# Reordering the last two expert pairs of a one-core diffusion trunk step: one residual on GpSimd, early return tiles, a split output tile

## The chip, the cores and the metric

The kernel runs on one core of a Trainium2 chip. A core has TensorE (matrix products into the eight banks of PSUM), VectorE, ScalarE, GpSimd and SyncE, each with its own queue of instructions, and 16 DMA engines that move data between the chip's memory and SBUF. The engines meet only at semaphores: an instruction raises one when it is done, and a wait in another queue holds that queue, and everything behind it, until the count is reached. The metric is the device time of one execution in microseconds, as the median of several runs; a profile is one execution more.

## The reference

One layer of a trunk over 384 tokens of width 1024: 128 context tokens and 256 latent tokens, each with its own condition. A mixer block (Fourier branch and retention branch) comes first, then the mixture of experts with which the changed code has to do, then a last norm:

```
x = x + g1 * mix
h = rmsnorm(x, norm2_g) * (1 + sc2) + sh2
x = x + g2 * moe(h)          # 64 experts of width 256, 8 chosen per token, and a shared one
y = rmsnorm(x, final_norm_g)
```

Here `g2` is a row of 1024 gates, one row for the context tokens and one for the latent tokens. An expert computes `(silu(t @ we_g) * (t @ we_u)) @ we_d` for the tokens that chose it, times their routing weight. All 64 experts are computed, and their weights (3 MB each) are read once. The outputs are `y` for both sets of tokens and the two retention states of the context.

## The kernel before

The tokens are three tiles of 128 rows (`TT = 3`): tile 0 is the context, tiles 1 and 2 are the latent tokens. `x` holds them in SBUF, 128 x 3 x 1024. The mixer and the routing take the first 370 us or so. Then the 64 experts go by in 32 pairs (`PAIRS = LAST = 32`, so the last two are pairs 30 and 31). The order of every engine's queue is written out by hand.

For a pair `p`, GpSimd gathers the tokens' rows from memory, TensorE turns them, and `gate_up(p)` multiplies them with the gate and up weights into bank 0. ScalarE takes the silu, VectorE multiplies it with the up half and the routing weight (`hidden`, `hid_ready`), TensorE turns the hidden rows into bank 1 (`hidden_T`), ScalarE copies them to SBUF (`hidT_ready`), and `down(p)` makes two halves of 512 columns in banks 2 and 3. The rows then go back to their tokens by products with a one-hot matrix `slotT`. So that this is exact enough, a row is split into a rounded high part `y_hi` (ScalarE, `hi_ready`) and a remainder `y_lo` (VectorE, `lo_ready`), and each of six return tiles (three token tiles, two column halves) is the sum of two matmuls, one for each part. For pairs 0 to 29 VectorE adds the six return tiles to `y_sum`, a buffer in `hTf` (`sums`, `summed`).

The last two pairs go another way. GpSimd gathers each slot's gate row (`gather_gates`), VectorE multiplies the down product with it (`remainder_gated`, which also forms the remainders), and the return tiles of both pairs accumulate in six banks (`LAST_BANKS = (4, 5, 6, 7, 0, 1)`, in the order of `LAST_TILES`: the three tiles' low halves, then their high halves). The last adds then go straight to `x` (`last_sums`). What pairs 0 to 29 left in `y_sum` is multiplied by the gate rows and added to `x` by `residual(t)`, two VectorE operations of 128x1024 for each token tile. The gate rows come by a DMA of SyncE's queue (`g2_rows_in`) behind the last weights.

The order on TensorE at the end is `gate_up(31)`, `hidden_T(31)`, the return of pair 30 (`scatter_two(30)`), `down(31)`, the return of pair 31 (`scatter_two(31)`). On VectorE it is `residual(0)`, the pair's weights, `hidden(31)`, `residual(1)`, `residual(2)`, `remainder_gated(31)`, then a load of the number of further rounds from SBUF with a branch on it (there are none for these inputs, so the `Else` side runs), `last_sums`, and `final_norm(t)` for each tile. ScalarE computes the squares for the norm as the sums come. SyncE writes a tile of 512 KB as soon as `out_ready` says that it is normalised. GpSimd, after the last gathers, loads the final gains into `fin_g`, once pair 30's gated halves are done with the buffer.

In the profile's rows the names are those of the buffers: `bank` is PSUM, `hT` holds `y_sum`, `U` the gate rows, `QK` and `AB` the two gated halves (and `AB` later the final gains), `VG` the hidden rows, `Fm` the slots' gate rows of pair 31.

Of the kernel before, what the change touches and what calls it, by code (L numbers as in the profile page):

```python
# [224 lines left out]
def trunk_kernel(nc, A, outs, consts, dists):  # L225
    y_prompt, y_sample, new_f, new_b = outs
    ctx = ExitStack()
    with ctx:
# [163 lines left out]
        slot_gate = {LAST - 2: AB1[:, 0:1024], LAST - 1: Fm[:, 2048:3072]}  # L392
        base_3 = small[:, 304:307]
# [135 lines left out]
        def _(sp):  # L529
# [106 lines left out]
            for t in range(TT):  # L636
                sp.wait_ge(sem("out_ready"), t + 1)
                dst = y_prompt[0, :, :] if t == 0 else y_sample[0, (t - 1) * P:t * P, :]
                sp.dma_start(dst, x[:, t, :]).then_inc(sem("out_written"), 16)
            sp.wait_ge(sem("out_written"), 16 * TT)  # L640
# [8 lines left out]
        def _(pool):  # L649
# [86 lines left out]
            for p in range(2, LAST):  # L736
# [6 lines left out]
                if p in slot_gate:  # L743
                    gather_gates(p)
            pool.wait_ge(sem("y_gated"), 2)
# [15 lines left out]
        def _(pe):  # L761
# [612 lines left out]
            def scatter_two(p):  # L1374
                first = p == LAST - 2
                if first:
                    pe.wait_ge(sem("summed"), 6 * p)
                for n, (t, h) in enumerate(LAST_TILES):
                    if n == 0 or not first and n == 3:
                        pe.wait_ge(sem("lo_ready"), 2 * p + (2 if first or n else 1))  # L1380
                    if first and LAST_BANKS[n] == 1:
                        pe.wait_ge(sem("hidT_ready"), LAST)
                    o = ps[LAST_BANKS[n]][:, :]
                    for i, y in enumerate((y_hi, y_lo)):
                        ins = mm(o, slotT[p % KEEP][:, t * P:(t + 1) * P], y[:, h * 512:(h + 1) * 512], start=(first and i == 0), stop=(not first and i == 1))
                    ins.then_inc(sem("scattered"), 1)
# [22 lines left out]
            gate_up(LAST - 1)  # L1409
            hidden_T(LAST - 1)  # L1410
            scatter_two(LAST - 2)
            down(LAST - 1)
            scatter_two(LAST - 1)
# [308 lines left out]
        def _(dve):  # L1722
# [571 lines left out]
            def remainder_gated(p):  # L2294
                j = p - (LAST - 2)
                dve.wait_ge(sem("gates_in"), 16 * (j + 1))
                for h in range(2):
# [5 lines left out]
                for h in range(2):  # L2303
                    cut = slice(h * 512, (h + 1) * 512)
                    dve.wait_ge(sem("hi_ready"), 2 * p + h + 1)
                    v.tensor_tensor(y_lo[:, cut], y_gated[h], y_hi[:, cut], ALU.subtract).then_inc(sem("lo_ready"), 1)

# [35 lines left out]
            def residual(t):  # L2343
# [4 lines left out]
                else:  # L2348
                    dve.wait_ge(sem("x_formed"), t)
# [135 lines left out]
```

## Time and profile before

| | us |
|---|---|
| median of 3 runs | 895.19 |
| lowest, highest | 893.06, 895.57 |
| the profiled execution | 895.6 |
| its span (first to last instruction) | 893.8 |
| TensorE busy in the span | 868.0 (97%) |
| VectorE busy | 472.6 (53%) |
| ScalarE busy | 166.7 (19%) |
| GpSimd busy | 58.3 (7%) |

The profiled execution's own time is longer than its span by what lies before the first and behind the last instruction. The busy shares are means over the whole span and do not say what ends last; the stretch that the change touches is the last 30 us, and it is read engine by engine. Matmuls are pipelined: each starts before the one ahead of it has ended, so their starts, not their durations, give the pace. In a row of a timeline, the brackets give the engine's idle time ahead of the instruction and what ended it.

### The profile page before, as it was taken

The numbers are of one execution on the slowest core, as the hardware profiler recorded it, in microseconds if no ns is written. First come the engines' busy times: TensorE is split into PE (matmuls) and PEld (weight loads), VectorE is DVE, ScalarE is ACT, GpSimd is POOL, SyncE is SP. The second block draws the span as 40 slices with busy tenths as digits, with TensorE's granted clock in tenths as the row PEclk, the third lists the DMA queues.
The fourth block names the chain that finished last, engine by engine and source line by source line (L and its number), as shares of the span: only waits on it lengthen the run. The fifth ranks groups of instructions, "written<-read, shape, count | busy, mean of one in ns | idle before, by whom it ended". The sixth has DMA issues, their size and how long they took to land.

```text
span 893.8 us, 11385 instructions
## 1 busy us (share of the span) xinstructions
PE 868.0 (97%) x4186; PEld 445.6 (50%) x4186; DVE 472.6 (53%) x1031; ACT 166.7 (19%) x349; POOL 58.3 (7%) x75
## 2 busy tenths in 40 slices
PE   7999999999999999999999999999999999999884
PEld 6774446777655547644544444434444444444332
DVE  3645398936796945434443444435444353535447
ACT  4131012020000034121111112112121212111113
POOL 1020100000000000100000000000000000000000
PEclk9999999999999999999999999999999999999998
DMA  9998433512575847499999999999999999999981
GB/s 330 389 368 226 148 125 126 197 50 92 224 279 201 352 192 259 162 408 419 421 418 419 417 419 417 418 418 409 412 421 418 421 418 421 418 420 418 418 328 74
DMA packets 63626, 288.00 MB, mean 322 GB/s; under 512 B 6472, under 2 KB 6528, under 8 KB 38480
## 3 DMA queue, kind: packets, MB, share of 16 engines
q1 hardware_dynamic: 56176, 265.60, 74.8%
q0 software_dynamic: 7392, 21.63, 6.5%
q8 instruction: 35, 0.57, 0.3%
q14 instruction: 23, 0.19, 0.1%
HBM read 287.34 MB, written 4.33 MB: 326 GB/s over the span
## 4 chain that ended last, share of the span: by engine, by line
PE 89%; DMA 8%; DVE 2%; SPq 1%; issue 1%; ACT 0%; DVEq 0%
PE bank L1270 23%; PE bank L834 12%; PE bank L1295 11%; PE bank L827 9%; PE bank L1313 9%; DMA ring<-in_w_exp_up 6%; PE bank L1051 5%; DMA ring<-in_w_ada 2%; PE bank L1212 2%; PE bank L1098 1%; PE bank L1215 1%; PE bank L839 1%; PE bank L844 1%; PE bank L1311 1%; PE bank L1004 1%; PE bank L1006 1%
## 5 line engine op out<-in xcount | busy, mean ns | idle before, releaser
L1270 PE MATMUL bank<-ring,QK 128*64 128x512 f32 (+1 forms) x1056 | 228.3, 602 | 5.8 <-DMA ring<-in_w_exp_up 5.8
L2286 DVE TENSOR_TENSOR hT<-bank,hT 128x512 f32<-128x512 f32 x174 | 109.7, 684 | 83.1 <-PE bank L1313 82.2
L1270 PEld LDWEIGHTS bank<-ring,QK 128*64 128x64 f32 (+1 forms) x1056 | 71.4, 130 | 128.3 <-issue 128.3
L2275 DVE SCALAR_TENSOR_TENSOR VG<-VG,cw,bank 128x256 f32<-128x256 f32 x32 | 15.4, 480 | 170.9 <-issue 164.9
L1295 PE MATMUL bank<-ring,VG 128*64 128x512 f32 (+1 forms) x512 | 102.2, 598 | 0.4 <-ACT VG L1656 0.4
L834 PE MATMUL bank<-hT,ring 128*128 128x384 f32 x256 | 86.0, 489 | 0.0
L827 PE MATMUL bank<-ring,hT 128*128 128x512 f32 x192 | 82.7, 593 | 0.0
L1313 PE MATMUL bank<-y_hi,slotT 128*128 128x512 f32 x180 | 80.9, 449 | 0.0
L1313 PE MATMUL bank<-y_lo,slotT 128*128 128x512 f32 x180 | 70.9, 394 | 0.0
L1663 ACT CAST y_hi<-bank 128x512 fp32r<-128x512 f32 x60 | 32.3, 589 | 195.2 <-PE bank L1313 191.9
L834 PEld LDWEIGHTS bank<-hT,ring 128*128 128x128 f32 x256 | 47.8, 190 | 33.7 <-issue 2.4
L827 PEld LDWEIGHTS bank<-ring,hT 128*128 128x128 f32 x192 | 36.4, 190 | 45.7 <-issue 45.7
L1295 PEld LDWEIGHTS bank<-ring,VG 128*64 128x64 f32 (+1 forms) x512 | 29.4, 130 | 58.3 <-issue 57.8
L1270 PE MATMUL bank<-spare,QK 128*64 128x512 f32 x128 | 56.6, 595 | 0.0
L1313 PEld LDWEIGHTS bank<-y_hi,slotT 128*128 128x128 f32 x180 | 33.8, 188 | 30.7 <-issue 25.7
L1645 ACT ACTIVATE VG<-bank 128x256 f32<-128x256 f32 x32 | 12.3, 385 | 196.3 <-PE bank L1270 196.3
L1051 PE MATMUL bank<-ring,U 128*128 128x512 f32 x96 | 42.0, 593 | 0.0
L2292 DVE TENSOR_TENSOR y_lo<-bank,y_hi 128x512 fp32r<-128x512 f32 x60 | 38.5, 682 | 3.6 <-ACT y_hi L1663 3.5
L1313 PEld LDWEIGHTS bank<-y_lo,slotT 128*128 128x128 f32 x180 | 34.0, 189 | 7.8 <-issue 2.9
L1650 ACT COPY QK<-bank 128x512 f32<-128x512 f32 x62 | 33.3, 589 | 5.6 <-PE bank L1212 5.5
L645 POOL DMA_INDIRECT QK<-h_rows,idx x16 | 15.9, 992 | 218.8 <-DVE idx L2191 190.8
L645 POOL DMA_INDIRECT VG<-h_rows,idx x16 | 16.1, 1005 | 215.3 <-DVE idx L2191 200.2
(425 smaller groups left out, 950.4 us busy)
## 6 DMA issues: line engine op xcount, KB each, us to landing
ring<-in_w_exp_gate SPq DMA_DIRECT2D x56, 1024.0 KB, 12.3
ring<-in_w_exp_up SPq DMA_DIRECT2D x56, 1024.0 KB, 15.1
ring<-in_w_exp_down SPq DMA_DIRECT2D x56, 1024.0 KB, 17.0
ring<-in_w_ada SPq DMA_DIRECT2D x12, 2048.0 KB, 12.2
ring<-in_w_in SPq DMA_DIRECT2D x9, 2048.0 KB, 18.0
spare<-in_w_exp_gate SPq DMA_DIRECT2D x8, 1024.0 KB, 11.2
spare<-in_w_exp_up SPq DMA_DIRECT2D x8, 1024.0 KB, 14.4
spare<-in_w_exp_down SPq DMA_DIRECT2D x8, 1024.0 KB, 18.7
```

The lines of the kernel that those rows point to most:

```text
L645: pool.indirect_dma_start(xg[n], None, h2_rows, bass.IndirectOffsetOnAxis(idx[:, k:k + 1], 0), bounds_check=T - 1, oob_is_err=False).then_ ...
L827: ins = mm(o[:, :], h[:, k, t * P:(t + 1) * P], w[:, k, :], start=(k == 0), stop=(k == KC - 1))
L834: ins = mm(o[:, 0:T], w[:, k, m * P:(m + 1) * P], rhs[:, k, :], start=(k == 0), stop=(k == kc - 1))
L1051: ins = mm(o[:, :], mergedT[:, k, t * P:(t + 1) * P], w[:, k, :], start=(k == 0), stop=(k == KC - 1))
L1212: ins = nc.tensor.transpose(lo[:, k * P:(k + 1) * P], xg[n][:, k * P:(k + 1) * P], ident)
L1270: ins = mm(ps[0][rows, :], xT[:, k, rows], gate_up_of(p, n)[:, k, :, :], start=(k == 0), stop=(k == KC - 1))
L1295: ins = mm(ps[2 + h][rows, :], hidT[:, j, rows], down_of(p, n)[:, j, h * 512:(h + 1) * 512], start=(j == 0), stop=(j == 1))
L1313: ins = mm(o, slotT[k][:, t * P:(t + 1) * P], y[:, h * 512:(h + 1) * 512], start=(n == 0 and not shared), stop=(n == 1))
L1650: nc.scalar.copy(halves[n], ps[4 + n][:, :].rearrange("p (k s) -> p k s", k=4)).then_inc(sem("xT_ready"), 1)
L1663: nc.scalar.copy(y_hi[:, h * 512:(h + 1) * 512], ps[2 + h][:, :]).then_inc(sem("hi_ready"), 1)
L2286: v.tensor_tensor(into, o, into, ALU.add).then_inc(sem("summed"), 1)
L2292: v.tensor_tensor(y_lo[:, cut], ps[2 + h][:, :], y_hi[:, cut], ALU.subtract).then_inc(sem("lo_ready"), 1)
```

## The change

Four things are changed.

- The residual of token tile 2 is no longer VectorE's. GpSimd does its multiplication and its addition, after the gate rows have landed and `summed` shows the sums complete, and before it loads the final gains. VectorE waits for the result (`pool_formed`) at its third last sum.
- The return of pair 30 is cut in two. Its first three tiles stand ahead of `hidden_T(31)` in TensorE's queue, the other three behind it. The return of pair 31 is written as `scatter_last`: for each column half first the three matmuls with the high rows, which wait only for `hi_ready`, then the three with the remainders.
- In `remainder_gated`, pair 31 forms its first remainder between the two gatings, no longer behind both. Pair 30 keeps its order.
- The last output tile is normalised and written in two halves of 512 columns.

The counter `sum_gated` goes, and `x_formed` counts two steps for each tile in its place.

```diff
@@ -390,6 +390,7 @@
         fin_g = AB1[:, 0:1024]
         y_gated = [QK[:, 1536:2048], AB1[:, 1024:1536]]
         slot_gate = {LAST - 2: AB1[:, 0:1024], LAST - 1: Fm[:, 2048:3072]}
+        out_cuts = [[slice(0, D)], [slice(0, D)], [slice(0, 512), slice(512, D)]]
         base_3 = small[:, 304:307]
         ssq_low = small[:, 307:310]
 
@@ -633,11 +634,11 @@
                     load_item(q * 2 + (2 + n), n, load_down, "down_next", 16)
 
             further_rounds(sp, load_next, load_first)
-            for t in range(TT):
-                sp.wait_ge(sem("out_ready"), t + 1)
-                dst = y_prompt[0, :, :] if t == 0 else y_sample[0, (t - 1) * P:t * P, :]
-                sp.dma_start(dst, x[:, t, :]).then_inc(sem("out_written"), 16)
-            sp.wait_ge(sem("out_written"), 16 * TT)
+            for n, (t, cut) in enumerate((t, cut) for t in range(TT) for cut in out_cuts[t]):
+                sp.wait_ge(sem("out_ready"), n + 1)
+                dst = y_prompt[0, :, cut] if t == 0 else y_sample[0, (t - 1) * P:t * P, cut]
+                sp.dma_start(dst, x[:, t, cut]).then_inc(sem("out_written"), 16)
+            sp.wait_ge(sem("out_written"), 16 * sum(len(cuts) for cuts in out_cuts))
 
 
         def gather(pool, n, k, landed):
@@ -742,6 +743,12 @@
                 gather(pool, p % 2, p % KEEP, f"gathered{p % 2}")
                 if p in slot_gate:
                     gather_gates(p)
+            pool.wait_ge(sem("g2_rows_in"), 16)
+            pool.wait_ge(sem("summed"), 6 * (LAST - 2))
+            sum_2 = hTf[:, 2 * D:3 * D]
+            nc.gpsimd.tensor_tensor(sum_2, sum_2, g2_rows[:, 1, :], ALU.mult).then_inc(sem("pool_formed"), 1)
+            pool.wait_ge(sem("pool_formed"), 1)
+            nc.gpsimd.tensor_tensor(x[:, 2, :], x[:, 2, :], sum_2, ALU.add).then_inc(sem("pool_formed"), 1)
             pool.wait_ge(sem("y_gated"), 2)
             pool.dma_start(fin_g, A["final_norm_g"].rearrange("(o n) -> o n", o=1).broadcast_to([P, D])).then_inc(sem("fin_in"), 16)
 
@@ -1371,19 +1378,31 @@
                         pe.wait_ge(sem("summed"), 6 * p + g - 3)
                     scatter_tile(p, g, FREE_FIRST)
 
-            def scatter_two(p):
-                first = p == LAST - 2
-                if first:
+            def return_part(p, n, y, start, stop):
+                t, h = LAST_TILES[n]
+                return mm(ps[LAST_BANKS[n]][:, :], slotT[p % KEEP][:, t * P:(t + 1) * P], y[:, h * 512:(h + 1) * 512], start=start, stop=stop)
+
+            def scatter_next_to_last(tiles):
+                p = LAST - 2
+                if 0 in tiles:
                     pe.wait_ge(sem("summed"), 6 * p)
-                for n, (t, h) in enumerate(LAST_TILES):
-                    if n == 0 or not first and n == 3:
-                        pe.wait_ge(sem("lo_ready"), 2 * p + (2 if first or n else 1))
-                    if first and LAST_BANKS[n] == 1:
+                    pe.wait_ge(sem("lo_ready"), 2 * p + 2)
+                for n in tiles:
+                    if LAST_BANKS[n] == 1:
                         pe.wait_ge(sem("hidT_ready"), LAST)
-                    o = ps[LAST_BANKS[n]][:, :]
-                    for i, y in enumerate((y_hi, y_lo)):
-                        ins = mm(o, slotT[p % KEEP][:, t * P:(t + 1) * P], y[:, h * 512:(h + 1) * 512], start=(first and i == 0), stop=(not first and i == 1))
-                    ins.then_inc(sem("scattered"), 1)
+                    return_part(p, n, y_hi, True, False)
+                    return_part(p, n, y_lo, False, False).then_inc(sem("scattered"), 1)
+
+            def scatter_last():
+                p = LAST - 1
+                for h in range(2):
+                    tiles = range(3 * h, 3 * h + 3)
+                    pe.wait_ge(sem("hi_ready"), 2 * p + h + 1)
+                    for n in tiles:
+                        return_part(p, n, y_hi, False, False)
+                    pe.wait_ge(sem("lo_ready"), 2 * p + h + 1)
+                    for n in tiles:
+                        return_part(p, n, y_lo, False, True).then_inc(sem("scattered"), 1)
 
             slots_of(2)
             gate_up(0)
@@ -1407,10 +1426,11 @@
                 down(p)
                 scatter(p - 1, range(4, 6))
             gate_up(LAST - 1)
+            scatter_next_to_last(range(3))
             hidden_T(LAST - 1)
-            scatter_two(LAST - 2)
+            scatter_next_to_last(range(3, 6))
             down(LAST - 1)
-            scatter_two(LAST - 1)
+            scatter_last()
 
             def further(q):
                 p = q + LAST
@@ -2294,16 +2314,25 @@
             def remainder_gated(p):
                 j = p - (LAST - 2)
                 dve.wait_ge(sem("gates_in"), 16 * (j + 1))
-                for h in range(2):
+                def gated(h):
                     cut = slice(h * 512, (h + 1) * 512)
                     dve.wait_ge(sem("down_done"), 2 * p + h + 1)
                     if j:
                         dve.wait_ge(sem("lo_ready"), 2 * p)
                     v.tensor_tensor(y_gated[h], ps[2 + h][:, :], slot_gate[p][:, cut], ALU.mult).then_inc(sem("y_gated"), 1)
-                for h in range(2):
+
+                def low(h):
                     cut = slice(h * 512, (h + 1) * 512)
                     dve.wait_ge(sem("hi_ready"), 2 * p + h + 1)
                     v.tensor_tensor(y_lo[:, cut], y_gated[h], y_hi[:, cut], ALU.subtract).then_inc(sem("lo_ready"), 1)
+
+                gated(0)
+                if j:
+                    low(0)
+                gated(1)
+                if not j:
+                    low(0)
+                low(1)
 
             def pair_weights(p):
                 dve.wait_ge(sem(f"gathered{p % 2}"), 16 * (p // 2 + 1))
@@ -2346,10 +2375,10 @@
                     dve.wait_ge(sem("g2_rows_in"), 16)
                     dve.wait_ge(sem("summed"), 6 * (LAST - 2))
                 else:
-                    dve.wait_ge(sem("x_formed"), t)
+                    dve.wait_ge(sem("x_formed"), 2 * t)
                 tile_sum = hTf[:, t * D:(t + 1) * D]
-                v.tensor_tensor(tile_sum, tile_sum, gate[t], ALU.mult).then_inc(sem("sum_gated"), 1)
-                dve.wait_ge(sem("sum_gated"), t + 1)
+                v.tensor_tensor(tile_sum, tile_sum, gate[t], ALU.mult).then_inc(sem("x_formed"), 1)
+                dve.wait_ge(sem("x_formed"), 2 * t + 1)
                 v.tensor_tensor(x[:, t, :], x[:, t, :], tile_sum, ALU.add).then_inc(sem("x_formed"), 1)
 
             for p in range(PAIRS):
@@ -2377,7 +2406,6 @@
                     v.tensor_tensor(s_hid[2], s_silu, s_hid[2], ALU.mult).then_inc(sem("third_ready"), 1)
                 if last:
                     residual(1)
-                    residual(2)
                 else:
                     sums(p - 1, FREE_FIRST)
                 if p in slot_gate:
@@ -2391,10 +2419,12 @@
 
             def last_sums(low, high):
 
-                dve.wait_ge(sem("x_formed"), TT)
+                dve.wait_ge(sem("x_formed"), 2 * (TT - 1))
                 for n, (t, h) in enumerate(LAST_TILES):
                     cut = slice(h * 512, (h + 1) * 512)
                     dve.wait_ge(sem("scattered"), 6 * (LAST - 1) + n + 1)
+                    if n == 2:
+                        dve.wait_ge(sem("pool_formed"), 2)
                     if n == 5 and low == "x2_low":
                         base()
                     v.tensor_tensor(x[:, t, cut], ps[LAST_BANKS[n]][:, :], x[:, t, cut], ALU.add).then_inc(sem(high if h else low), 1)
@@ -2428,8 +2458,8 @@
                 stand_alone(dve, "rounds_done")
                 for t in range(TT):
                     tile_sum = hTf[:, t * D:(t + 1) * D]
-                    v.tensor_tensor(tile_sum, tile_sum, gate[t], ALU.mult).then_inc(sem("sum_gated"), 1)
-                    dve.wait_ge(sem("sum_gated"), TT + t + 1)
+                    v.tensor_tensor(tile_sum, tile_sum, gate[t], ALU.mult).then_inc(sem("x_formed"), 1)
+                    dve.wait_ge(sem("x_formed"), 2 * (TT - 1) + t + 1)
                     v.tensor_tensor(x[:, t, :], x[:, t, :], tile_sum, ALU.add).then_inc(sem("x2_ready"), 1)
                     dve.wait_ge(sem("x2_ready"), t + 1)
 
@@ -2448,7 +2478,8 @@
             def final_norm(t):
                 dve.wait_ge(sem("std3"), t + 1)
                 link(v.reciprocal(rstd[:, t:t + 1], rstd[:, t:t + 1]))
-                v.scalar_tensor_tensor(x[:, t, :], x[:, t, :], rstd[:, t:t + 1], fin_g, ALU.mult, ALU.mult).then_inc(sem("out_ready"), 1)
+                for cut in out_cuts[t]:
+                    v.scalar_tensor_tensor(x[:, t, cut], x[:, t, cut], rstd[:, t:t + 1], fin_g[:, cut], ALU.mult, ALU.mult).then_inc(sem("out_ready"), 1)
 
             dve.wait_ge(sem("fin_in"), 16)
             for t in range(TT):
```

## Rows read from the trace of the kernel before

**Rows 1.** The chain of waits in order of time: start us, us, what

```profile
837.03 26.22 DMA ring<-in_w_exp_up
```

**Rows 2.** Windows of core 0: us, busy per engine, TensorE clock, DMA share, GB/s

```profile
872.15:873.31 1.16, 0.00 (x1) 0.03 (x1) 0.63 (x2) 0.38 (x1) 0.00 (x0) 1.00 0.02 7
```

**Rows 3.** Timeline of TensorE: start us, us, line, operation, [idle before <-what ended it]

```profile
863.38 8.77 PE L1270 MATMUL bank<-ring,QK 128*32 128x512 f32 x64 [2.60 <-DMA ring<-in_w_exp_up]
873.31 0.41 PE L1281 MATMUL bank<-consts_sb,VG 128*128 128x128 f32 x2 [1.16 <-DVE VG L2275]
...
873.79 0.39 PE L1385 MATMUL bank<-y_lo,slotT 128*128 128x512 f32 x1
...
876.08 0.39 PE L1385 MATMUL bank<-y_lo,slotT 128*128 128x512 f32 x1
876.40 3.64 PE L1295 MATMUL bank<-ring,VG 128*32 128x512 f32 x32
```

**Rows 4.** Timeline of VectorE (DVE), from pair 30's last remainder to the last sums

```profile
863.53 0.68 DVE L2306 TENSOR_TENSOR y_lo<-AB,y_hi 128x512 fp32r<-128x512 f32 x1
867.03 1.22 DVE L2351 TENSOR_TENSOR hT<-hT,U 128x1024 f32<-128x1024 f32 x1 [2.82 <-DMA U<-mod_rows]
...
869.43 0.28 DVE L2312 SCALAR_TENSOR_TENSOR VG<-consts_sb,expert_at,QK 128x64 f32<-128x64 f32 x1
...
872.68 0.48 DVE L2275 SCALAR_TENSOR_TENSOR VG<-VG,cw,bank 128x256 f32<-128x256 f32 x1 [2.97 <-issue]
...
874.33 1.23 DVE L2353 TENSOR_TENSOR x<-x,hT 128x1024 f32<-128x1024 f32 x1
...
876.85 1.22 DVE L2353 TENSOR_TENSOR x<-x,hT 128x1024 f32<-128x1024 f32 x1
878.45 0.69 DVE L2302 TENSOR_TENSOR QK<-bank,Fm 128x512 f32<-128x512 f32 x1 [0.37 <-PE bank L1295]
880.11 0.69 DVE L2302 TENSOR_TENSOR AB<-bank,Fm 128x512 f32<-128x512 f32 x1 [0.97 <-PE bank L1295]
880.72 0.68 DVE L2306 TENSOR_TENSOR y_lo<-QK,y_hi 128x512 fp32r<-128x512 f32 x1
881.49 0.69 DVE L2306 TENSOR_TENSOR y_lo<-AB,y_hi 128x512 fp32r<-128x512 f32 x1
882.69 2.50 DVE L2400 TENSOR_TENSOR x<-bank,x 128x512 f32<-128x512 f32 x4 [0.51 <-PE bank L1385]
```

**Rows 5.** Timeline of ScalarE (ACT) in the same stretch

```profile
873.75 0.37 ACT L1656 COPY VG<-bank 128x256 f32<-128x256 f32 x1 [1.16 <-PE bank L1281]
879.17 0.62 ACT L1675 CAST y_hi<-QK 128x512 fp32r<-128x512 f32 x1 [5.05 <-DVE QK L2302]
880.84 0.62 ACT L1675 CAST y_hi<-AB 128x512 fp32r<-128x512 f32 x1 [1.04 <-DVE AB L2302]
```

**Rows 6.** Line 2437 on VectorE's sequencer (DVEq): ns min/median/max, first and last start us

```profile
L2437 DVEq TENSOR_LOAD <-DT x1: 542/542/542, 881.5 to 881.5; - x1
```

**Rows 7.** Timeline of GpSimd (POOL), its last instruction

```profile
863.13 0.57 POOL L746 DMA_DIRECT2D AB<-in_final_norm_g  x1 [8.59 <-DVE AB L2302]
```

**Rows 8.** Memsets of lines 2470 (GpSimd) and 2402 (VectorE): ns min/median/max, starts

```profile
L2470 POOL MEMSET const-float32-0.0<- x1: 92/92/92, 0.2 to 0.2; 128x1 f32 x1
...
L2470 POOL MEMSET const-uint8-127<- x1: 110/110/110, 0.3 to 0.3; 128x1 uint8 x1
...
L2402 DVE MEMSET small<- x1: 59/59/59, 884.5 to 884.5; 128x1 f32 x1
```

**Rows 9.** DMA issues by line: count, KB each, median us from issue to landing

```profile
AB<-in_final_norm_g POOLq DMA_DIRECT2D x1, 512.0 KB, 8.4
```

**Rows 10.** Window of the three output transfers, columns as in rows 2

```profile
888.80:893.00 4.20, 0.00 (x0) 0.00 (x0) 1.90 (x3) 0.00 (x0) 0.00 (x0) 0.50 0.93 375
```

**Rows 11.** Groups of VectorE by line and shape, 860 to 894: busy us, mean ns, idle before

```profile
L2451 DVE SCALAR_TENSOR_TENSOR x<-x,small,AB 128x1024 f32<-128x1024 f32 x3 | 3.9, 1284 | 0.1
L2400 DVE TENSOR_TENSOR x<-bank,x 128x512 f32<-128x512 f32 x6 | 3.8, 684 | 0.5 <-PE bank L1385 0.5
```

## The prediction

> **What bounds the kernel now.** I read the chain of waits first. Its one long link near the end is the load of the last gate and up weights [rows 1]; until that load lands, at about 863.3 us, TensorE works at the pace of the weights, and nothing in the diff changes a weight load. So the change can act only on the roughly 30 us after it, and I read those engine by engine: TensorE's timeline [rows 3], VectorE's [rows 4], ScalarE's [rows 5], VectorE's sequencer [rows 6] and the transfers that write the output [rows 10].
>
> Those 30 us are a relay. The gate and up product of pair 31 runs from 863.38 to 872.15 [rows 3]. TensorE then stands still for 1.16 us [rows 2, 3], while ScalarE and VectorE make the hidden rows, because the turning of those rows is next in its queue and waits for them. Then come the turning, twelve return matmuls of pair 30 and, at 876.40, the down product. From there VectorE leads: it gates the two halves (878.45, 880.11), forms the two remainders (880.72, 881.49), and sums from 882.69 [rows 4]. The first sum is held by VectorE itself and not by the matmuls: behind the second remainder its sequencer loads the count of further rounds, at 881.5 for 0.54 us, and branches on it before the sums [rows 6]. The 1.20 us from 881.49 to 882.69 therefore move with that remainder. After 882.69 sums and norms follow one another, and each output tile leaves when normalised.
>
> **The change part by part.**
>
> *Three return tiles ahead of the turning.* Their inputs are long there: the second remainder of pair 30 ends at 864.21 [rows 4]. Six matmuls step by 0.229 us (873.79 to 876.08 is ten steps), and the first of a run costs about 0.1 more, since 0.48 us pass from the turning at 873.31 over one return to the next at 873.79 [rows 3]. Begun at the end of the gate and up product, the six fill 872.15 to 873.62 (6 x 0.229 + 0.1). The hidden rows' product starts at 872.68 and the turning 0.63 us later [rows 3, 4], so the rows are ready by then. The turning at 873.62, 0.48 us to the second return behind it, four steps of 0.229 and 0.32 us to the down product (876.08 to 876.40) give 875.34 in place of 876.40. The sixth tile waits for ScalarE's copy of the turned rows; that copy ends 0.81 us after the turning starts [rows 3, 5], and the four matmuls ahead of the tile last longer. The down weights don't stop this: in the idle stretch the DMA engines are busy for 2% [rows 2], so practically all has landed by 872.15. **Term: -1.1 us.**
>
> *Third tile's residual to GpSimd.* VectorE today runs two residuals from 873.1 to 878.07 and is free 0.37 us before the gating at 878.45 [rows 4]. With the down product at 875.3 the gating could start at 877.4, and a second residual on VectorE would eat 0.7 us of the gain. With one alone, VectorE is free at 875.56. The move earns nothing by itself and lets the first term through. Its own cost is on GpSimd, whose two operations wait for the gate rows (used by VectorE at 867.03). The trace has no such operation on GpSimd. The same work on VectorE costs 1.22 us each [rows 4], the bound below. For the other bound I scale that by the nearest pair of like operations: a memset of 128x1 takes 92 to 110 ns on GpSimd and 59 on VectorE [rows 8], which makes 1.9 to 2.3 us each. At 2.3 both end at 871.6, some 11 us before the third sum wants the result. The load of the final gains is now queued behind them on GpSimd; it was issued at 863.13 [rows 7] and needed 8.4 us beside the weights [rows 9]. Issued at 871.6 it lands by 880.6 even at that price, before the sums begin. **Term: 0**, if the two engines run beside each other. The nearest row for that is GpSimd's issue at 863.13, 0.57 us long, which overlaps a VectorE subtraction of 0.68 us with two SBUF inputs; the like subtractions at 880.72 and 881.49, with GpSimd idle, take 0.68 and 0.69 [rows 4, 7]. An issue isn't a tensor operation, so exclusion stays a rival below.
>
> *Order of the last gated rows.* Now: gate 0, gate 1, remainder 0, remainder 1. Then: gate 0, remainder 0, gate 1, remainder 1. Remainder 0 waits for ScalarE's cast, which starts 0.72 us after gate 0 and takes 0.62 [rows 4, 5], and then starts 0.04 later; gate 1 follows by a spacing of 0.61 (880.11 to 880.72). So gate 1 starts 1.99 us after gate 0, where it now starts 1.66 after (when the second half of the down product is done). The second cast and remainder 1 follow as before, and the load, the branch and the first sum with them. What TensorE gains by taking the high rows early is not used, for no sum can start before the branch. **Term: +0.33 us** on the path.
>
> *Split output tile.* Each norm takes 1.28 us [rows 11], and from 888.80 to 893.00 the DMA engines are busy for 93% [rows 10]: three tiles of 1.40 us each, without a hole. The first half is issued some 0.6 us sooner, but then waits behind tile 1; its 0.7 us and those of the second half fill the same 1.40 us. Were the queue empty, the split would give 0.70 (half of 1.40) less what two norms cost more. A half of 512 costs 1.28 less 0.54 (1.22 less 0.68, the two lengths of a tensor operation [rows 4, 11]), so 0.74; two of them, overlapped by the 0.07 that 0.68 exceeds the spacing of 0.61, make 1.41, 0.13 more. Gain between 0 and 0.57; I take **0**, because the rows show no hole to move into.
>
> The renamed counters leave VectorE the same number of waits per tile; the added wait of the third sum has nothing left to wait for.
>
> **Sum:** -1.06 + 0 + 0.33 + 0 = -0.73 us. The profiled execution took 895.6 us (893.8 of span and 1.8 around it), so 894.9 by its own time. It lies 0.4 us above the median of the runs shown, 895.19; I give the forecast against the median: **894.5**.
>
> **The rivals.**
>
> *The two engines exclude each other (other side).* Between the landing of the gate rows and the hidden product VectorE has two residual operations and the pair weights; they end at 869.71 [rows 4]. If GpSimd's two operations of length c each shut it out in turn, that becomes 869.71 + 2c. The turning at 873.62 needs the hidden product's start by 872.99, so the loss is 2c - 3.28 us: 0.5 at c = 1.9 (895.0), 1.3 at c = 2.3, which turns the whole into +0.6 (895.8, slower than now). It decides the sign from c = 2.0, and passes 0.3% (2.7 us, about what a measurement of this kernel can tell from no change) from c = 3.4. For it: both engines are released by the same landing. Against it: the undisturbed subtraction above, and that the pair weights may slip in ahead of the second operation, which leaves the hidden product untouched.
>
> The Trainium skill speaks for this rival: SBUF — State Buffer, section Who interferes with whom, says that a VectorE operation with two SBUF inputs contends with a GpSimd operation that reads SBUF, and that the one which starts first holds the shared port for its whole instruction. No run so far shows it. GPSIMD Engine Reference, section 3.1, gives an addition of this kind 1.96 times VectorE's time on GpSimd; by that, as an estimate, c would be 2.4 us and the sum about +0.8 us.
>
> *The split pays in full.* If the queue has room after all, 0.57 us more: -1.3 us, 893.9. Against it stands the 93%.
>
> *The early returns win nothing.* If something holds them until the hidden rows are made, only the longer order is left: +0.33, 895.5. All their inputs are there 8 us before, so little speaks for it.
>
> **How the numbers follow.** Forecast 0.47; exclusion 0.33 (0.05 of it with c above 3.4); split 0.10; early returns 0.04; an effect outside these (other code on every queue) 0.06, in both directions. All named cases but long exclusion lie within 2.7 us of now. Faster by over 0.3%: 0.04; within: 0.89; slower: 0.07. The range holds the forecast and the rivals from 893.9 to 895.8, and beyond them the spread of single runs, 893.06 to 895.57, about whose median the new one may fall by about 1 us: 892.8 to 896.2.
>
> **What would show it.** In the profile of the changed kernel: returns between the gate and up product and the turning, and no idle of 1.16 us; the down product 3.2 us after the end of the gate and up product instead of 4.25; gate 1 about 2.0 us after gate 0; the first sum 6.6 us after the start of the down product instead of 6.3; the output transfers still back to back; VectorE's first residual at 1.22 us an operation with GpSimd beside it. Wrong would make me: a hidden product later than 873.0 against a product end of 872.15, GpSimd operations above 3.4 us, a sum that waits for them, or a hole ahead of the last half tile.

## The result, and the profile after

The changed kernel takes 897.25 us (median of 22 runs) against 894.88 for the kernel before: a ratio of 1.0027, 95% interval 1.0017 to 1.0037, so 2.4 us slower. The forecast was 894.5 us, in a range of 892.8 to 896.2. The other terms of the sum came out as worked out, in the runs that try them one by one below; the one taken as 0, GpSimd beside VectorE, turned the sign, and its consequence for TensorE's clock had not been priced at all.

GpSimd's and VectorE's timelines of the changed kernel, to be read beside [rows 4] and [rows 7] (line numbers are those of the changed kernel):

```profile
867.61 2.37 POOL L749 TENSOR_TENSOR hT<-hT,U 128x1024 f32<-128x1024 f32 x1 [12.44 <-DMA U<-mod_rows]
870.07 3.23 POOL L751 TENSOR_TENSOR x<-x,hT 128x1024 f32<-128x1024 f32 x1
873.25 0.61 POOL L753 DMA_DIRECT2D AB<-in_final_norm_g  x1
```

```profile
867.62 3.45 DVE L2380 TENSOR_TENSOR hT<-hT,U 128x1024 f32<-128x1024 f32 x1 [2.79 <-DMA U<-mod_rows]
871.10 3.28 DVE L2382 TENSOR_TENSOR x<-x,hT 128x1024 f32<-128x1024 f32 x1
874.31 0.27 DVE L2341 SCALAR_TENSOR_TENSOR VG<-consts_sb,expert_at,QK 128x64 f32<-128x64 f32 x1
...
874.62 0.48 DVE L2295 SCALAR_TENSOR_TENSOR VG<-VG,cw,bank 128x256 f32<-128x256 f32 x1
875.02 1.22 DVE L2380 TENSOR_TENSOR hT<-hT,U 128x1024 f32<-128x1024 f32 x1
...
880.58 0.69 DVE L2322 TENSOR_TENSOR QK<-bank,Fm 128x512 f32<-128x512 f32 x1 [3.08 <-PE bank L1302]
881.95 0.69 DVE L2327 TENSOR_TENSOR y_lo<-QK,y_hi 128x512 fp32r<-128x512 f32 x1 [0.68 <-ACT y_hi L1695]
...
882.56 0.68 DVE L2322 TENSOR_TENSOR AB<-bank,Fm 128x512 f32<-128x512 f32 x1
883.93 0.69 DVE L2327 TENSOR_TENSOR y_lo<-AB,y_hi 128x512 fp32r<-128x512 f32 x1 [0.69 <-ACT y_hi L1695]
885.14 2.50 DVE L2430 TENSOR_TENSOR x<-bank,x 128x512 f32<-128x512 f32 x4 [0.52 <-issue]
```

Both engines are released by the same landing, within 0.01 us. The same VectorE operation that takes 1.22 us at 875.02 is drawn 3.45 us long at 867.62: 2.37 us of GpSimd's multiplication, then its own work. GpSimd's addition follows, 3.23 us long, of which the first 1.0 lies under the end of VectorE's operation; VectorE's addition then waits again, 3.28 us. A blocked operation has no gap in front of it in such a view. It looks busy, and only its length against its twin tells. The two operations of the first residual together take 4.28 us more than their 2.45, and the hidden product starts at 874.62, where the prediction had named a start later than 873.0 as a sign that it was wrong. The silu that it needs was there 3.5 us earlier (its end is at 871.08), since the gate and up product took only 7.07 us in this execution:

```profile
863.56 7.07 PE L1277 MATMUL bank<-ring,QK 128*32 128x512 f32 x64 [2.16 <-DMA ring<-in_w_exp_up]
870.56 0.50 PE L1383 MATMUL bank<-y_hi,slotT 128*128 128x512 f32 x1
...
871.83 0.40 PE L1383 MATMUL bank<-y_lo,slotT 128*128 128x512 f32 x1
875.25 0.50 PE L1288 MATMUL bank<-consts_sb,VG 128*128 128x128 f32 x2 [3.03 <-DVE VG L2295]
...
875.97 0.63 PE L1383 MATMUL bank<-y_lo,slotT 128*128 128x512 f32 x1
876.40 0.63 PE L1383 MATMUL bank<-y_hi,slotT 128*128 128x512 f32 x1
...
878.24 3.92 PE L1302 MATMUL bank<-ring,VG 128*32 128x512 f32 x32
```

That is TensorE's timeline of the changed kernel (compare [rows 3]). The three early tiles lie where they were meant to, right behind the product. Then TensorE idles for 3.03 us, and the return matmuls behind the turning step by 0.43 us and not by 0.229. The windows of this stretch (columns as in [rows 2]) say why:

```profile
872.20:875.25 3.05, 0.02 (x1) 0.03 (x1) 3.02 (x5) 0.00 (x0) 1.66 (x2) 1.00 0.08 32
875.25:878.24 2.99, 2.99 (x8) 1.97 (x8) 2.21 (x2) 0.38 (x1) 0.00 (x0) 0.53 0.35 142
```

The granted clock is 0.53 behind the idle stretch, so nearly all of it at the lower of the two levels (1.2 GHz). Turning to down product takes 2.99 us where 1.72 were worked out, and the first half of the down product 2.34 us to the gating where it was 2.05.

Counted to the first sum (882.69 before, 885.14 now), the two profiles differ by 2.45 us: forecast -0.73; turning at 875.25 and not at 873.62, +1.63; slow return matmuls, +1.27; slow start of the down product, +0.29; together +2.46. From the first sum to the end of the span nothing has changed: 11.11 us before, 11.06 now.

That this meets the 2.4 us of the medians is in part luck, for the two executions differ in one thing more: the gate and up product took 8.77 us in the profile before and 7.07 in this one, and both lengths come up whatever the change (see the last experiment). In the changed kernel the shorter product wins nothing, because the hidden product waits for VectorE. The chain of waits of this profile (start, us, what) runs over the landing of the gate rows, and no longer over the last up weights as in [rows 1]:

```profile
838.97 28.57 DMA U<-mod_rows
```

A fairer comparison is the kernel with the split output tile alone (below), which up to the last norm runs in the order of the kernel before and whose product was short too. Its product and its first sum:

```profile
863.18 7.07 PE L1271 MATMUL bank<-ring,QK 128*32 128x512 f32 x64 [2.51 <-DMA ring<-in_w_exp_up]
880.80 2.50 DVE L2416 TENSOR_TENSOR x<-bank,x 128x512 f32<-128x512 f32 x4 [0.51 <-PE bank L1377]
```

From the start of the product to the first sum it takes 17.62 us, and the changed kernel 21.58: with the short product the change costs 3.96 us. Against the long one of the profile before (19.31 us from 863.38 to 882.69) the same 21.58 are 2.27 more; no profile shows the changed kernel with the long product. The medians stand for both kinds of execution together.

### The profile page after: what moved, and what is told of

Same layout as the page of the kernel before. It is cut to its first block, busy times and chain, and to the rows that moved or that the text cites. A ratio compares the mean times of both kernels' runs of the same rounds, so it can differ in the third digit from the quotient of the medians.

```text
span 896.2 us, 11391 instructions
## 1 busy us (share of the span) xinstructions
PE 870.4 (97%) x4186; PEld 447.1 (50%) x4186; DVE 474.6 (53%) x1030; ACT 166.7 (19%) x349; POOL 63.9 (7%) x77
## 4 chain that ended last, share of the span: by engine, by line
PE 87%; DMA 8%; DVE 2%; issue 1%; SPq 1%; ACT 1%; DVEq 0%
PE bank L1277 23%; PE bank L841 12%; PE bank L1302 11%; PE bank L834 9%; PE bank L1320 9%; PE bank L1058 5%; DMA U<-mod_rows 3%; DMA ring<-in_w_exp_up 3%; DMA ring<-in_w_ada 2%; PE bank L1219 2%; PE bank L1105 1%; PE bank L1222 1%; PE bank L846 1%; PE bank L851 1%; PE bank L1318 1%; PE bank L1011 1%
```

## The experiments

Theory: a GpSimd tensor operation shuts VectorE's operations with two SBUF inputs out, and TensorE's clock falls in the stall that follows. Rivals: the new order of the gated rows costs the time; or the cut return does; or the slow matmuls have another cause than the idle stretch. Each ratio is against the kernel before on the same chip, with its 95% interval.

**Third residual back on VectorE, the rest of the change kept.**

```diff
-            nc.gpsimd.tensor_tensor(sum_2, sum_2, g2_rows[:, 1, :], ALU.mult).then_inc(sem("pool_formed"), 1)
-            nc.gpsimd.tensor_tensor(x[:, 2, :], x[:, 2, :], sum_2, ALU.add).then_inc(sem("pool_formed"), 1)
...
                     residual(1)
+                    residual(2)
```

> The changed kernel with the third tile's residual back on VectorE, the other three parts kept. Theory (GpSimd's two operations and VectorE's first residual shut each other out, and the hidden product waits): the hidden product starts as soon as the silu is there, the first residual takes 1.22 us an operation again, and nearly all of the loss goes: about 0.5 us to either side of the kernel before (early returns -1.06, of which the third residual on VectorE eats 0.7, order +0.33). Rival (the order of the last gated rows and the cut return cost the time): still 2 us or more above the kernel before.

Measured 0.9998 (0.9989 to 1.0006). The loss is gone with GpSimd's two operations. The first residual takes 1.23 and 1.22 us again. VectorE's first gating and first sum, with the down product at 874.07:

```profile
876.78 0.68 DVE L2316 TENSOR_TENSOR QK<-bank,Fm 128x512 f32<-128x512 f32 x1
881.33 2.50 DVE L2423 TENSOR_TENSOR x<-bank,x 128x512 f32<-128x512 f32 x4 [0.51 <-issue]
```

The gating follows the down product by 2.71 us and not by 2.05, since VectorE has the third residual to do first, and the first sum follows by 7.26.

**GpSimd's residual alone, in the kernel before.**

```diff
+            nc.gpsimd.tensor_tensor(sum_2, sum_2, g2_rows[:, 1, :], ALU.mult).then_inc(sem("pool_formed"), 1)
+            nc.gpsimd.tensor_tensor(x[:, 2, :], x[:, 2, :], sum_2, ALU.add).then_inc(sem("pool_formed"), 1)
...
                     residual(1)
-                    residual(2)
```

> The kernel before with one part of the change: the third tile's residual on GpSimd. Theory: slower than before by 2 to 3 us, with VectorE's two operations of the first residual above 3 us each and the hidden product 2 us or more behind the silu. Rival (GpSimd's part is harmless by itself and only meets the early returns badly): within 0.7 us of before or faster.

Measured 1.0061 (1.0043 to 1.0080), some 5 us slower: worse than the whole change, and more than expected. VectorE's two operations:

```profile
867.27 3.46 DVE L2373 TENSOR_TENSOR hT<-hT,U 128x1024 f32<-128x1024 f32 x1 [2.64 <-DMA U<-mod_rows]
870.76 3.25 DVE L2375 TENSOR_TENSOR x<-x,hT 128x1024 f32<-128x1024 f32 x1
```

Without early tiles the stall is idle from end to end, and all twelve return matmuls come behind it, as the windows show:

```profile
870.70:874.87 4.17, 0.00 (x1) 0.03 (x1) 4.10 (x6) 0.38 (x1) 2.78 (x2) 1.00 0.16 63
874.87:879.55 4.68, 4.68 (x15) 3.46 (x15) 2.21 (x2) 0.38 (x1) 0.00 (x0) 0.64 0.17 65
```

From the turning to the down product the kernel before takes 3.09 us ([rows 3], 873.31 to 876.40) and this one 4.68, so 1.6 of the 5 us are the clock. That part was missing in the expectation. The stall itself is 4.17 us in place of 1.16 [rows 2], 3.0 more (the product took 7.07 us here).

**Early return tiles alone.**

```diff
+            scatter_next_to_last(range(3))
             hidden_T(LAST - 1)
-            scatter_two(LAST - 2)
+            scatter_next_to_last(range(3, 6))
```

> The kernel before with one part of the change: three return tiles of pair 30 ahead of the turning; all residuals on VectorE, old order, whole last tile. Theory: the idle of 1.16 us ahead of the turning goes, the down product starts 1.06 us sooner against the end of the gate and up product, but VectorE's third residual holds the first gating, so that 0.3 to 0.5 us are gained. Rival (early returns cost TensorE time of their own): equal or slower than before.

Measured 0.9991 (0.9974 to 1.0007): not clear of no change by time. By the rows of its profile the expectation was too low. VectorE's timeline, with the down product at 873.27, 3.14 us behind the end of the gate and up product at 870.13:

```profile
874.84 1.22 DVE L2370 TENSOR_TENSOR x<-x,hT 128x1024 f32<-128x1024 f32 x1
875.98 0.68 DVE L2313 TENSOR_TENSOR QK<-bank,Fm 128x512 f32<-128x512 f32 x1
876.98 0.69 DVE L2313 TENSOR_TENSOR AB<-bank,Fm 128x512 f32<-128x512 f32 x1 [0.31 <-PE bank L1296]
...
879.55 2.50 DVE L2417 TENSOR_TENSOR x<-bank,x 128x512 f32<-128x512 f32 x4 [0.51 <-PE bank L1377]
```

The third residual does hold the first gating, to 2.71 us behind the down product in place of 2.05. But in the old order the second gating waits for TensorE anyway (0.31 us idle ahead of it), and the first sum comes 6.28 us behind the down product, as before (6.29). In this order the residual that was moved to GpSimd costs nothing on VectorE.

**GpSimd's residual later: behind VectorE's two.**

```diff
-            pool.wait_ge(sem("g2_rows_in"), 16)
-            pool.wait_ge(sem("summed"), 6 * (LAST - 2))
+            pool.wait_ge(sem("x_formed"), 2 * (TT - 1))
```

> The changed kernel with GpSimd's two operations held until VectorE's two residuals are done. Theory (exclusion, and only against VectorE operations with two inputs in SBUF): the hidden product is on time and the first residual takes 1.22 us an operation; the gatings, which read PSUM and one input in SBUF, keep 0.69 us beside GpSimd; the first remainder, with two inputs in SBUF, is held by GpSimd's second operation by up to 1.7 us. Between 0.5 us faster and 1 us slower than before. Rival (GpSimd slows every VectorE operation): the gating beside GpSimd takes over 1.5 us as well. Rival (no exclusion by time, the slow part is elsewhere): the time of the changed kernel.

Measured 1.0008 (0.9997 to 1.0019). The hidden product is on time: it starts 0.53 us behind the end of the gate and up product, as before. The run also shows which operations are shut out, in the timelines of GpSimd and VectorE:

```profile
875.22 2.38 POOL L748 TENSOR_TENSOR hT<-hT,U 128x1024 f32<-128x1024 f32 x1 [18.45 <-DVE x L2381]
877.68 2.37 POOL L750 TENSOR_TENSOR x<-x,hT 128x1024 f32<-128x1024 f32 x1
```

```profile
876.93 0.69 DVE L2321 TENSOR_TENSOR QK<-bank,Fm 128x512 f32<-128x512 f32 x1 [1.80 <-PE bank L1301]
878.30 2.29 DVE L2326 TENSOR_TENSOR y_lo<-QK,y_hi 128x512 fp32r<-128x512 f32 x1 [0.69 <-ACT y_hi L1694]
```

The gating (one input in PSUM, one in SBUF) lies beside GpSimd's multiplication and takes its 0.69 us. The remainder (both inputs in SBUF) starts under GpSimd's addition and ends 0.5 us behind it, 2.29 us long in place of 0.69. The rival that GpSimd slows every VectorE operation has fallen. So has one that was not named: the remainder (`QK`, `y_hi`, `y_lo`) and GpSimd's addition (`x`, `hT`) share no buffer, so it isn't a clash over one buffer that holds it.

**The changed kernel with eight idle matmuls in the stall.**

```diff
             scatter_next_to_last(range(3))
+            for _ in range(8):
+                mm(ps[7][:, :], slotT[(LAST - 2) % KEEP][:, 0:P], y_hi[:, 0:512], start=True, stop=True)
             hidden_T(LAST - 1)
```

> The changed kernel with eight idle return matmuls more (1.8 us of them, into a bank that is begun anew afterwards) between the early return tiles and the turning, so that TensorE does not stand still while the hidden product waits for VectorE. Theory (part of the loss is TensorE's clock, which falls after the long idle stretch): the hidden product is as late as in the changed kernel, but the return matmuls behind the turning step by 0.23 us and not by 0.43, the down product starts 1.7 us after the turning in place of 3.0, and 1 to 1.5 us are won against the changed kernel. Rival (the slow steps come from GpSimd or VectorE at the port, not from the idle stretch): the steps stay at 0.43 and the time is that of the changed kernel or longer.

Measured 1.0011 (1.0000 to 1.0022), against 1.0027 for the changed kernel. VectorE's two operations are as long as ever (3.46 and 3.30 us), but TensorE's idle stretch is 1.00 us, and behind it the windows show the full clock:

```profile
872.12:873.12 1.00, 0.01 (x2) 0.04 (x1) 0.96 (x5) 0.00 (x0) 0.00 (x0) 1.00 0.60 160
873.12:874.85 1.73, 1.73 (x8) 1.19 (x8) 1.70 (x2) 0.38 (x1) 0.00 (x0) 1.00 0.58 211
```

Turning to down product takes 1.73 us and not 2.99. So the slow matmuls came from TensorE's standing still, and more work made this stretch 1.26 us shorter. By time it is some 1.4 us (1.0027 less 1.0011); the two ratios are from two chips and their intervals overlap.

**The order of pair 31's gated rows and return alone** (VectorE's part; on TensorE `scatter_last` as in the change).

```diff
                 gated(0)
+                if j:
+                    low(0)
                 gated(1)
+                if not j:
+                    low(0)
                 low(1)
```

> The kernel before with one part of the change: gate, remainder, gate, remainder for pair 31, and TensorE's high rows first. Theory: the second gating 1.99 us after the first in place of 1.66, the first sum 6.62 us after the start of the down product in place of 6.29, 0.3 us slower than before. Rival (TensorE's earlier high rows bring the sums forward): faster than before.

Measured 0.9999 (0.9988 to 1.0011). In its profile the second gating starts 1.98 us after the first (876.89), and the first sum 6.61 us after the down product (874.84):

```profile
878.87 0.68 DVE L2315 TENSOR_TENSOR AB<-bank,Fm 128x512 f32<-128x512 f32 x1
881.45 2.50 DVE L2422 TENSOR_TENSOR x<-bank,x 128x512 f32<-128x512 f32 x4 [0.51 <-issue]
```

The +0.33 us is in the rows; by time it is below what can be told.

**The split output tile alone.**

```diff
+        out_cuts = [[slice(0, D)], [slice(0, D)], [slice(0, 512), slice(512, D)]]
...
-                v.scalar_tensor_tensor(x[:, t, :], x[:, t, :], rstd[:, t:t + 1], fin_g, ALU.mult, ALU.mult).then_inc(sem("out_ready"), 1)
+                for cut in out_cuts[t]:
+                    v.scalar_tensor_tensor(x[:, t, cut], x[:, t, cut], rstd[:, t:t + 1], fin_g[:, cut], ALU.mult, ALU.mult).then_inc(sem("out_ready"), 1)
```

> The kernel before with one part of the change: the last output tile normalised and written in halves. Theory (the output transfers stand back to back): the two norms take 0.13 us more together, the second half's transfer ends where the whole tile's did, 0 to 0.1 us to either side. Rival (the half pays in full): 0.57 us faster.

Measured 1.0000 (0.9991 to 1.0009): nothing, as the full queue had it. The same shows in the changed kernel, the last norms and the window of its four output transfers (see [rows 10, 11]):

```profile
891.90 1.42 DVE L2482 SCALAR_TENSOR_TENSOR x<-x,small,AB 128x512 f32<-128x512 f32 x2
```

```profile
891.30:895.40 4.10, 0.00 (x0) 0.00 (x0) 1.98 (x4) 0.00 (x0) 0.00 (x0) 0.50 0.95 377
```

The two halves take 1.42 us (1.41 worked out), the DMA engines are busy for 95% of 4.1 us, and the last half has no hole to move into.

**GpSimd's residual timed into VectorE's idle stretch.**

```diff
-            pool.wait_ge(sem("g2_rows_in"), 16)
-            pool.wait_ge(sem("summed"), 6 * (LAST - 2))
+            pool.wait_ge(sem("weights_ready"), 2 * LAST)
```

> The changed kernel with GpSimd's two operations held until the weights of pair 31 are formed on VectorE, so that the first of them falls into VectorE's idle stretch ahead of the hidden product, which itself has one input in SBUF. Theory (exclusion): the first residual takes 1.22 us an operation and the hidden product is on time; GpSimd's first operation takes 2.37 us; VectorE's second residual meets its second one and is held by up to 2.4 us, which costs the first gating 0 to 1.2 us. 0.7 us faster than before to 0.5 us slower. Rival (GpSimd's work is too slow anywhere): as the changed kernel, 2 us or more slower than before.

Measured 1.0001 (0.9991 to 1.0012). One wait is another, and the change's loss is gone with GpSimd doing the same work. The two timelines:

```profile
868.54 2.38 POOL L748 TENSOR_TENSOR hT<-hT,U 128x1024 f32<-128x1024 f32 x1 [15.25 <-DVE VG L2340]
871.00 2.40 POOL L750 TENSOR_TENSOR x<-x,hT 128x1024 f32<-128x1024 f32 x1
```

```profile
865.76 1.23 DVE L2379 TENSOR_TENSOR hT<-hT,U 128x1024 f32<-128x1024 f32 x1 [2.82 <-DMA U<-mod_rows]
...
871.02 0.48 DVE L2294 SCALAR_TENSOR_TENSOR VG<-VG,cw,bank 128x256 f32<-128x256 f32 x1 [2.57 <-issue]
871.42 3.06 DVE L2379 TENSOR_TENSOR hT<-hT,U 128x1024 f32<-128x1024 f32 x1
```

The hidden product (one input in PSUM) is on time beside GpSimd's addition, 0.53 us behind the end of the gate and up product; only the second residual is held, by 1.8 us, and it has slack: the first gating still starts 2.05 us behind the down product (875.67 and 873.62).

**Residuals around the hidden product, all on VectorE, with early return tiles.**

```diff
                 pair_weights(p)
+                if last:
+                    residual_gated(0)
+                    residual_added(0)
+                    residual_gated(1)
...
                 if last:
-                    residual(1)
-                    residual(2)
+                    residual_added(1)
+                    residual_gated(2)
+                    residual_added(2)
```

> The kernel before with the early return tiles, and with VectorE's residuals laid around the hidden product: the pair's weights first, the first residual and the second one's multiplication ahead of it, the rest behind it. Nothing on GpSimd, old order of the gated rows, whole last tile. Theory (VectorE had room ahead of the hidden product, the move to GpSimd was not needed): the first gating starts 2.05 us after the down product, undelayed, and the whole early term is kept: 1.0 us faster than before. Rival (the multiplication moved ahead delays the hidden product): no gain.

Measured 0.9986 (0.9975 to 0.9997), 1.2 us faster. The first gating starts 2.05 us behind the down product (877.01 and 874.96). But the first sum (881.25) follows the down product by 6.29 us, where early return tiles alone had 6.28, and the two ratios, 0.9986 and 0.9991, can't be told apart. The gain is that of the early tiles; that the new order of the residuals adds to it is not shown.

**The same, with the load of the round count taken ahead.**

```diff
+                    n_rounds = dve.value_load(tab_rounds, min_val=0, max_val=FURTHER)
                     residual_gated(0)
...
-            dve.wait_ge(sem("table_ready"), 1)
-            n_rounds = dve.value_load(tab_rounds, min_val=0, max_val=FURTHER)
             with dve.If(n_rounds > 0):
```

> As the run before, with the load of the number of further rounds taken from behind the second remainder to the start of VectorE's last pair; the branch stays. Theory (the first sum is held by that load): the first sum starts about 0.75 us after the second remainder in place of 1.20, then with the first return tile, and 0.4 us more is gained: 1.4 to 1.5 us faster than before. Rival (the matmuls hold the first sum): the same time as the run before.

Measured 0.9988 (0.9977 to 1.0000): not to be told from the run before. In the profile the first sum does follow the second remainder by 0.81 us in place of 1.20 (876.90 and 877.71), so that the load did hold it. But ScalarE's first square starts at 878.70, 0.3 us behind the end of the first sum, because its table load and the small operation behind it end only at 878.66; part of the 0.4 us is given back there. How much is left is open.

**The same, with ten idle matmuls ahead of the last gate and up product.**

```diff
+            pe.wait_ge(sem("hid_ready"), LAST - 1)
+            kept = slotT[(LAST - 2) % KEEP]
+            for _ in range(10):
+                mm(ps[0][:, 0:T], kept[:, 0:P], kept, start=True, stop=True)
             gate_up(LAST - 1)
```

> The version with early return tiles, residuals around the hidden product and the load taken ahead, with ten idle matmuls more (1.7 us, into bank 0 before its product is begun) in the stretch in which TensorE waits for the last weights. Theory (in part of the executions the last gate and up product runs at half clock for some 4 us, after that wait): the product takes 7.07 us always, never 8.77, and 1 to 1.5 us are won on the mean against the version without them: 2.5 us (0.3%) faster than before. Rival (the slow stretch has another cause, or the idle matmuls run past the landing of the weights): no gain on the version without them, 1.2 us faster than before.

Measured 0.9973 (0.9963 to 0.9983): the fastest version, by that ratio 2.4 us faster than before where 2.5 was expected (the medians, 892.04 and 894.04 us, are 2.0 apart). TensorE's timeline:

```profile
859.10 1.93 PE L1422 MATMUL bank<-slotT 128*128 128x384 f32 x10
861.75 7.07 PE L1271 MATMUL bank<-ring,QK 128*32 128x512 f32 x64 [0.72 <-DMA ring<-in_w_exp_up]
```

The product took 8.77 us in the kernel before [rows 3] and in three other profiles of this study, and 7.07 in the rest. The mean granted clock over the 8.77 us before (863.38 to 872.15) is 0.81, that over the 7.07 us of the kernel with the split output tile is 1.00. With the idle stretch ahead of it cut to 0.72 us it took 7.07. One profile alone wouldn't show that the 8.77 is gone, for it came in only some of them; the time agrees with it, 1.3 us below the version without the ten matmuls (0.9988 less 0.9973), but from two chips and with intervals that overlap, so that the gain of these ten is not shown beyond doubt.

## Why the prediction was wrong

- **Early return tiles, -1.06: right.** In the runs without GpSimd's part the down product starts 3.10 to 3.14 us after the end of the gate and up product (worked out: 3.19; before: 4.25).
- **GpSimd's residual, 0: the step that failed.** The prediction took the two engines as running beside each other, by a row that was too far: GpSimd's issue of a DMA beside a VectorE subtraction. That row was of no tensor operation, as the prediction itself said, and it was trusted all the same: a chance of 0.47 for the forecast, 0.33 for exclusion. The rival with the other sign was the case, and its own parts held: operations of 2.37 us (just above the bound of 1.9 to 2.3 from the memsets), a price of twice that less the slack. At c = 2.37 the rival's formula gives a turning 1.46 us late; the profile shows 1.63, with the gate rows landing 0.6 us later and an overlap of some 0.5 us given back. The slack in that formula, 3.28 us, was read beside a product of 8.77 us; beside one of 7.07 it is 1.70 less and the price as much higher, which the prediction did not see. The Trainium skill, SBUF — State Buffer, section Who interferes with whom, states the rule that the rows show: 3.45 us for a VectorE operation with two SBUF inputs beside a GpSimd operation that reads SBUF, 0.69 for one with an input in PSUM. The Trainium skill, GPSIMD Engine Reference, section 3.1, gave the ratio behind the estimate of 2.4 us, which the trace meets with 2.37.
- **What a stall does to TensorE, not in the sum at all.** The rival was priced as lost time alone. Behind 3.03 us of standing still the clock was 0.53, which cost 1.56 us more in this execution (1.27 and 0.29). If it stands for the median, this is what carried the time out of the range: 897.25 less 1.56 is 895.7, inside. With the stall filled the steps are fast again.
- **The cover of the third residual, 0.7: right for the new order, wrong for the old one.** In the order before, with the early tiles, the second gating waits for TensorE, and the third residual on VectorE costs nothing. In the new order the second gating stands behind the first remainder, and it does cost: with the residual back on VectorE the first sum comes 7.26 us behind the down product (881.33 and 874.07), and not 6.62. The change created the need that its first part was there to meet.
- **Order of the gated rows, +0.33: right**, 6.61 us to the first sum (6.62 by the sum) in the run with this part alone.
- **Split output tile, 0: right**, by a ratio of 1.0000.

## What to carry to other kernels

An operation that goes to another engine is not free because that engine is idle: ask first which operations of the old engine it will run beside, whether the two shut each other out, and what ends the wait if they do. Here the same work was harmless beside operations with an input in PSUM and beside one that had slack, and cost 2 us or more when it met the two that the hidden product waits for. A stall of TensorE is to be priced twice, as time and as the clock of what comes after it. And before two profiles are subtracted, see whether they differ in something that the change didn't do, as here in the length of the gate and up product.

## What the runs showed of the hardware

In all three kernels with the full clash (the changed one, GpSimd's part alone, and the one with idle matmuls in the stall) both engines were released within 0.01 us of each other and GpSimd's operation went first, and then they took turns; whether that holds elsewhere is open. A VectorE operation that is shut out is recorded from its release, so its wait is inside its length (3.45 us for 1.22 of work). TensorE idle for 1.00 and 1.16 us kept the full clock afterwards (the run with idle matmuls in the stall, and [rows 2, 3]); after 3.03 us it was 0.53 over the next 2.99 us, and after 4.17 us 0.64 over the next 4.68; after waits of 2.2 to 2.8 us for the last weights both were seen, the product behind them taking 7.07 us in some profiles (clock 1.00) and 8.77 in others (0.81). What decides between the two is open.
